# Lead pairs of a decoder step's dense stages: the token slice moved from the innermost to the outermost loop of each part

## The reference, cut to what matters

```python
# layer 0: sparse attention heads + SSD heads, then
x = x + concat([o_nsa, o_ssm]) @ w_out_even        # output 0
h = rmsnorm(x, norm_ffn[0]); g, u = split(h @ w_gate_up[0])
x = x + (silu(g) * u) @ w_down[0]
# layer 1
h = rmsnorm(x, norm_mix[1]); q, kv = split(h @ w_in_odd)
x = x + sliding_window_attention(q, kv) @ w_out_odd # output 1
h = rmsnorm(x, norm_ffn[1]); g, u = split(h @ w_gate_up[1])
x = x + (silu(g) * u) @ w_down[1]
y = rmsnorm(x, norm_final)
```

## Time and profile before

| | |
|---|---|
| median of three runs | 2846.03 us |
| the profiled execution, its own time | 2842.67 us |
| its span (first to last instruction) | 2840.9 us |
| TensorE busy | 98% |
| weight loads busy | 89% |
| DVE, POOL, ACT busy | 36%, 26%, 23% |
| mean granted TensorE clock | 0.997 of full |

### The profile page before, as it was taken

How to read it: one execution, slowest core, us unless ns; L and a number is a source line. 1 busy time by engine, 2 the same in 40 slices (tenths; PEclk the granted TensorE clock), 3 DMA queues, 4 the chain that set the end, 5 groups by cost and what they waited for, 6 DMA issues and landing times.

```text
span 2840.9 us, 44686 instructions
## 1 busy us (share of the span) xinstructions
PE 2791.4 (98%) x18772; PEld 2535.5 (89%) x18772; DVE 1013.5 (36%) x2137; ACT 645.2 (23%) x1344; POOL 730.7 (26%) x495
## 2 busy tenths in 40 slices
PE   8999999999999999999999999999999999999999
PEld 6766676666689999999999999879999999999998
DVE  3122256776553322222222251383432222222224
ACT  4022214666542100000000031284200000000004
POOL 1430000212322222222222222244222222222221
PEclk9999999999999999999999999999999999999999
DMA  7754211110631111111111112100111111111111
GB/s 236 197 172 140 65 31 61 50 31 2 197 108 45 45 45 45 45 45 45 45 45 45 45 45 49 42 17 16 45 45 45 45 45 45 45 45 45 45 60 64
DMA packets 205898, 179.73 MB, mean 63 GB/s; under 512 B 36730, under 2 KB 186287, under 8 KB 205106
## 3 DMA queue, kind: packets, MB, share of 16 engines
q1 hardware_dynamic: 195184, 144.20, 17.1%
q0 software_dynamic: 7616, 30.14, 3.5%
q10 hardware_dynamic: 2898, 2.54, 0.3%
HBM read 162.44 MB, written 19.51 MB: 64 GB/s over the span
## 4 chain that ended last, share of the span: by engine, by line
PE 71%; DVE 2%; ACT 1%; issue 0%; POOL 0%; DVEq 0%; POOLq 0%; ACTq 0%
PE ps L2262 55%; PE ps L2298 4%; PE ps L2278 4%; PE ps L2966 1%; PE ps L2686 1%; PE ps L2546 1%; PE ps L2667 1%; PE ps L2650 1%; PE ps L1911 1%; PE ps L1899 1%; PE ps L1946 0%; DVE arena L2775 0%; DVE arena L2373 0%; PE ps L1928 0%; PE ps L2957 0%
## 5 line engine op out<-in xcount | busy, mean ns | idle before, releaser
L2262 PE MATMUL ps<-spot,w_hi 128*128 128x352 f32 (+1 forms) x6156 | 1520.5, 327 | 1.3 <-DVE arena L2389 0.7
L2262 PEld LDWEIGHTS ps<-spot,w_hi 128*128 128x128 f32 x6156 | 1083.0, 188 | 2.2 <-DVE arena L2389 1.3
L2262 PE MATMUL ps<-spot,w_lo 128*128 128x368 f32 (+1 forms) x3132 | 1019.9, 326 | 0.0
L2262 PEld LDWEIGHTS ps<-spot,w_lo 128*128 128x128 f32 x3132 | 588.8, 188 | 0.0
L2231 POOL CAST w_hi<-arena 128x2048 fp32r<-128x2048 f32 x78 | 150.5, 1930 | 1331.6 <-DMA arena<-in_w_gate_up 759.6
L2239 POOL TENSOR_TENSOR w_lo<-arena,w_hi 128x2048 fp32r<-128x2048 f32 x77 | 360.4, 4681 | 6.2
L2389 DVE TENSOR_TENSOR arena<-arena,ps 128x368 f32<-128x368 f32 (+1 forms) x312 | 147.2, 528 | 423.4 <-PE ps L2262 351.7
L601 PE MATMUL ps<-arena 128*128 128x368 f32 (+1 forms) x768 | 241.4, 473 | 0.0
L2487 ACT ACTIVATE arena<-arena 128x1088 f32<-128x1088 f32 x44 | 49.0, 1114 | 830.5 <-DVEq L2503 830.5
L601 PEld LDWEIGHTS ps<-arena 128*128 128x128 f32 x768 | 144.8, 191 | 86.1 <-issue 3.9
L2507 DVE TENSOR_TENSOR arena<-arena,ps 128x368 f32<-128x368 f32 x132 | 62.4, 528 | 442.6 <-PE ps L2262 437.5
(11 more groups left out here) (465 smaller groups left out, 3024.6 us busy)
## 6 DMA issues: line engine op xcount, KB each, us to landing
arena<-in_w_gate_up SPq DMA_DIRECT2D x88, 512.0 KB, 4.7
arena<-in_w_down SPq DMA_DIRECT2D x22, 1024.0 KB, 4.9
arena<-in_cache_nsa_slc_kv SPq DMA_DIRECT2D x112, 128.0 KB, 2.6
arena<-in_cache_nsa_cmp_kv SPq DMA_DIRECT2D x109, 128.0 KB, 2.3
arena<-in_w_in_even SPq DMA_DIRECT2D x9, 1024.0 KB, 7.6
x_spill<-arena POOLq DMA_DIRECT2D x1, 4352.0 KB, 14.1
arena<-in_x_prompt SPq DMA_DIRECT2D x8, 512.0 KB, 6.1
arena<-in_cmp_w_k POOLq DMA_DIRECT2D x16, 256.0 KB, 4.3
```

What stands on the lines that cost most here:

```text
L2262: mm = nc.tensor.matmul(ps[:, 3 * s + j, 0:b - a], w, x[:, a:b], start=m == 0, stop=m == len(order) - 1)
```

## The change

In `lead_pair` the loop over the slices `j` moves from inside the loop over the chunks to outside it, within each unit of each part. `before` is called for the first slice only, and `first` after the second matmul of the first slice. Nothing else differs.

```diff
                 for s in range(2):
                     if part == 0:
                         E.unit_start(s)
-                    for m, (kind, k) in enumerate(order):
-                        if s == 0:
-                            before(kind, k)
-                        (wh, wl), (xh, xl) = w_of(s, k), x_of(k)
-                        w, x = {"hh": (wh, xh), "hl": (wh, xl), "lh": (wl, xh)}[kind]
-                        for j, (a, b) in enumerate(SPLIT):
+                    for j, (a, b) in enumerate(SPLIT):
+                        for m, (kind, k) in enumerate(order):
+                            if s == 0 and j == 0:
+                                before(kind, k)
+                            (wh, wl), (xh, xl) = w_of(s, k), x_of(k)
+                            w, x = {"hh": (wh, xh), "hl": (wh, xl), "lh": (wl, xh)}[kind]
                             mm = nc.tensor.matmul(ps[:, 3 * s + j, 0:b - a], w, x[:, a:b], start=part == 0 and m == 0,
                                                   stop=part == 1 and m == KC - 1)
-                        if first and part == 0 and s == 0 and m == 1:
-                            first()
+                            if first and part == 0 and s == 0 and m == 1 and j == 0:
+                                first()
                     if part:
                         mm.then_inc(unit_ready[s], 1)
                     elif between:
                         between(s)
```

## The result

The changed kernel is slower: 2850.24 us, the median of twelve executions (2846.09 to 2865.49), against 2843.45 for twelve of the kernel before; the ratio is 1.0033, with a 95% interval of 1.0020 to 1.0046. That is +9.4 us (5.7 to 13.1), where +6.9 had been forecast. The ratio is not that of the two medians, which lie 6.8 us apart. The forecast time, 2852.9 us in a range of 2849.0 to 2856.5, stood on the median of three runs of the kernel before, 2846.03; the twelve put that kernel 2.6 lower.

A forecast was written before the change was run, and what follows sets the result against it. TensorE's own stream was taken to bound the kernel. Terms 4.3 + 0.6 + 0.54 - 0.3 + 0.6 = +5.7, plus 1.2 for the clock, made +6.9 on 2846.03: 2852.9 us, range 2849.0 to 2856.5.

The forecast's parts named there:

- TensorE's stream sets the time: Whole kernel: TensorE is busy 98% of the span, so time added to its stream counts in full unless it already waited.
- The step of 2.2 ns: Lead pairs: each matmul gains 2.2 ns where the old order steps 0.1667 us; 0.06 to 0.32 us per stage.
- Output 0, +4.3: Output 0's lead: 5.68 us of matmuls behind the last cast instead of 1.11, +4.57, less 0.09 and 0.17.
- The FFN leads, +0.6 each: FFN leads of both layers: third part waits for the eighth low chunk, +0.66, or +0.6 with the step gain.
- The high parts' 0.75: FFN leads: TensorE waits 0.75 us for the last high part's cast, free because it already waits for DVE's sum of squares.
- The projection, +0.54: First projection of layer 1: 0.75 us wait for the last high cast, uncovered, less 0.21 step gain.
- The clock, +1.2: Output 0: thin work makes the clock fall and slows dense work after the casts; +1.2 us, bounds 0 and 2.5.
- One, no price for the clock: Rival: late arrivals cost 5.7 us but the clock adds nothing, 2851.7 us; chance 0.22.
- Two, arrivals that do not bind: Rival: output 0's casts do not hold TensorE up, so not slower, 2847.3 or 2845.2 us; chance 0.14.
- Three, a second fall: Rival: clock falls more than once, FFN leads too, 2.5 us for output 0, 1 per other stall, 2855.7 us; chance 0.1.
- Four, weight reuse: Rival: neighbours no longer share a weight, 480 repeated loads exposed at 0.11 us each, +52, 2898 us; chance 0.01.

The follow-up runs named there:

- e6_arrivals: Kernel before, output 0 with both units taking each chunk in turn, slices outermost in output 1 and second units elsewhere, norm sums six matmuls later: ratio 1.0000.
- e3: Kernel before, with two slices inside the chunk loop and one behind it in the first unit's first part of output 0: ratio 1.0019.
- e5: Kernel before, with the new order only in the second unit of every lead pair, in both parts: ratio 0.9993.
- e2: Changed kernel with the old order back in output 0, so the new order stands in the other four lead pairs: ratio 1.0008.
- e7: Changed kernel with the old order in the first unit's low parts; executed once, 2850.82 us.
- e4: Changed kernel plus 18 unused matmuls, three behind each of chunks 1 to 6 of output 0's first slice: ratio 1.0013.
- e1: Kernel before with the new order in output 0 alone, the old one in the other four lead pairs: ratio 1.0032.

## Why the prediction was right, point by point

- **TensorE's stream sets the time.** Right. The stretches between the lead pairs kept their length (71.37 us behind output 0 in both kernels, 71.03 and 71.05 behind output 1), so nothing behind them gave back what they lost. The totals agree with the leads for the losses; the 3.4 us that e6_arrivals gained they are too coarse to show.
- **The step of 2.2 ns.** Right in kind, too large in sum: the plain units step as before (288 in 47.35 us from 953.75), and output 1, whose casts came in time, gained 0.36 (0.32 forecast). But the second units alone gave 0.53 us where 0.8 was expected, and output 0 nearly nothing where 0.17 was forecast: from the first start to the last of each piece, its second unit went from 166.1 to 165.3 ns a step, and its low parts from 166.0 to between 166.0 and 166.3. Nor is the step a matter of the order alone: the old order already stepped 164.4 ns in the second window of the earlier trace rows. Why it does so in one stretch and not in another is open.
- **Output 0, +4.3.** Right: 29.39 at full clock is +4.4. Behind the last arrival it is +4.57, the very figure of the sum; the casts ended 0.13 us sooner after the lead's start (0.09 forecast); the 0.17 of the step did not come. The half-way order confirms the rule by which it was worked out (2.24 against 2.23 behind the last arrival). The second unit started 13.5 us behind the first matmul at full clock, as forecast (824.8 - 811.4), and 15.7 with the fall.
- **The FFN leads, +0.6 each.** Right: +0.63 and +0.62, and for the reason given. The high parts' 0.75 went into the wait for the sums, which remained as 0.36 us between starts in place of 1.0.
- **The projection, +0.54.** Right where the clock was full: 28.48 in the kernel with fillers against 27.91, +0.57.
- **The clock, +1.2.** The fall came, the size was too small by half: 2.35 to 2.47 us in output 0, just under the upper bound of 2.5. The term that was mis-sized rests on the choice of a middle value because the thin work "lasts right up to the dense one". The clock did not come back when the dense work began but stayed low 5.1 us into it (831.2 to 836.3 in the changed kernel). In two of the three profiles the low stretch was 10.2 us long, where that of the earlier trace rows had been 3.4. That stretch was no sure sign either: the same work, unchanged, stands just ahead of output 0 in every kernel here, and a low stretch of 3.4 us stands in it in four of the nine profiles (before, the changed kernel, e3, e5).
- **A fall that was not forecast** stands in the projection's lead, 1.5 us a time, ahead of which PE runs 18 matmuls of one column; in the changed kernel:

```profile
1730.94 2.10 PE L2334 MATMUL ps<-ones,arena 128*128 128x1 f32 x18
```
```profile
1734.03:1737.44 3.41, 3.41 (x13) 3.41 (x12) 0.00 (x0) 2.28 (x6) 0.00 (x0) 0.50 0.62 173
```

These small matmuls stand in all nine kernels. The fall came in three of four profiles with the new order in the first unit there (the changed kernel, e2, e7, not e4) and in two of five with the old (e3, e6, not before, e1, e5). The order may make it likelier or not; nine profiles can't say, and it stays open.
- **The rivals.** One, no price for the clock, falls by the three low stretches. Two, arrivals that do not bind, falls by e1_out0_only. Three, a second fall, came near in size (+9.7 against +9.65 in the leads of the profile) but not in place: the FFN leads ran at full clock in every profile, and the second fall stood in the projection's lead, where it comes with the old order too. Four, weight reuse, falls by e5_second_unit_only: 360 of the 720 matmuls in the new order cost nothing.

With output 0 at 29.4 and its clock at 2.35, the terms make 4.4 + 2.35 + 0.63 + 0.57 - 0.36 + 0.62 = 8.2 us. The measured 9.4 (5.7 to 13.1) holds that. Without the clock they make 5.9 where 5.7 was forecast, so the mechanism and its sizes held, except for the clock. That the forecast +6.9 is also the distance of the two medians is luck: it has half the clock's price in it, and single executions of one kernel differ by some 20 us.

## What to carry to other kernels

Where a stage starts while its operands still arrive, what counts is how much work stands behind the last arrival: let each arrived chunk be used for all its slices before the next is waited for, and take slice after slice only where all chunks are there. A better step between matmuls (about 2 ns here) can't pay for slices left behind the last arrival (2.2 us for one, 4.6 for two). And thin, waiting work on TensorE has a second price, the clock that stays low after the wait is over; filling the gaps with unused matmuls removed that one here.

## What was not expected of the hardware

The length of the low stretches: 10.24, 10.24 and 6.83 us behind thin work in output 0.

And the FFN's wait for its sum of squares hangs on a near tie of two engines. DVE's last sum and POOL's weight cast begin close to each other in both FFNs. In 17 of the 18 cases of the nine profiles POOL's recorded start is 0.07 to 0.44 us ahead, and DVE's sum takes 2.98 or 2.99 us. In the FFN of layer 1 in e3_two_one it is 0.03 us ahead, and POOL's cast is the one that is stretched:

```profile
2056.87 1.28 DVE L2377 TENSOR_TENSOR arena<-arena,blocks 128x1088 f32<-128x1088 f32 x1
```
```profile
2056.84 3.06 POOL L2231 CAST w_hi<-arena 128x2048 fp32r<-128x2048 f32 x1 [17.41 <-DMA arena<-in_w_gate_up]
...
2059.98 5.54 POOL L2239 TENSOR_TENSOR w_lo<-arena,w_hi 128x2048 fp32r<-128x2048 f32 x1
```

DVE needed 1.28 us, POOL's cast 3.06 in place of 2.02, and TensorE did not wait for the sums: that lead took 25.83 us in place of 26.88, with no change to its order. By the Trainium skill (SBUF — State Buffer, "Who interferes with whom") the issue order decides which of VectorE and GpSimd blocks the other. The 17 cases agree; the one above neither confirms nor refutes it, since its two recorded starts are too close, and POOL's the earlier.
